# GpSimd's expert stage of a hybrid decoder layer written out for 64 experts, with index columns read in place

## The reference

```python
combine = jnp.einsum('tk,tke->te', gate, jax.nn.one_hot(expert_idx, N_EXPERTS, dtype=f32)).astype(x.dtype)
y = jnp.einsum('tf,fd->td', jax.nn.silu(xt @ ws_gate) * (xt @ ws_up), ws_down)
for c in range(N_EXPERTS // EXPERT_CHUNK):
    sl = slice(c * EXPERT_CHUNK, (c + 1) * EXPERT_CHUNK)
    g = jnp.einsum('td,edf->tef', xt, w_gate[sl])
    u = jnp.einsum('td,edf->tef', xt, w_up[sl])
    hdn = jax.nn.silu(g) * u * combine[:, sl, None]
    y = y + jnp.einsum('tef,efd->td', hdn, w_down[sl])
x = layer_norm(ALPHA * x + ffn + ple, ln2_g[i], ln2_b[i])
```

## Time and profile before

| | us |
|---|---|
| median of 3 runs | 1579.32 |
| lowest and highest run | 1578.99, 1583.84 |
| span of the profiled execution | 1578.7 |
| PE busy in it | 1434.9 |
| POOL busy in it | 463.6 |

### The profile page before, as it was taken

How to read it: one execution, slowest core, us unless ns; L and a number is a source line. 1 busy time by engine, 2 the same in 40 slices (tenths; PEclk the granted TensorE clock), 3 DMA queues, 4 the chain that set the end, 5 groups by cost and what they waited for, 6 DMA issues and landing times.

```text
span 1578.7 us, 18524 instructions
## 1 busy us (share of the span) xinstructions
PE 1434.9 (91%) x6293; PEld 938.1 (59%) x6293; DVE 858.9 (54%) x1240; ACT 600.2 (38%) x847; POOL 463.6 (29%) x414
## 2 busy tenths in 40 slices
PE   7979797988999999999975999999999999999990
PEld 4457676666788888554433666555555655556550
DVE  4597857674800100345614666656666566565654
ACT  3115454444622222010012554545545545455440
POOL 2012434343444444000351322223232222222322
PEclk8999898989899999999997999999999999999996
DMA  8034242425133335720156899999999999999953
GB/s 236 0 108 80 68 68 67 68 54 107 54 106 91 97 96 171 300 116 1 32 211 222 295 348 344 340 341 335 346 334 333 343 338 336 339 327 339 335 163 119
DMA packets 141491, 315.97 MB, mean 200 GB/s; under 512 B 18898, under 2 KB 100514, under 8 KB 116160
## 3 DMA queue, kind: packets, MB, share of 16 engines
q1 hardware_dynamic: 125984, 281.50, 51.8%
q0 software_dynamic: 15456, 33.79, 8.9%
HBM read 297.35 MB, written 34.65 MB: 210 GB/s over the span
## 4 chain that ended last, share of the span: by engine, by line
DMA 39%; PE 36%; issue 8%; DVE 5%; POOL 5%; ACT 2%; POOLq 2%; DVEq 1%; SPq 0%; ACTq 0%
DMA acc_dram<-arena 38%; PE bank L696 8%; PE bank L697 8%; PE bank L698 8%; PE bank L914 3%; PE bank L730 3%; POOL slot_dram L621 2%; DVE arena L1330 2%; PE bank L928 2%; PE bank L703 2%; POOL arena L643 2%; ACT arena L1111 1%; POOLq L587 1%; PE bank L829 1%; POOL arena L588 1%
## 5 line engine op out<-in xcount | busy, mean ns | idle before, releaser
L1330 DVE TENSOR_TENSOR gate_up_low<-gate_up,gate_up_high 128x1024 fp32r<-128x1024 f32 x256 | 296.4, 1221 | 228.6 <-ACT gate_up_high L1111 228.6
L1111 ACT ACTIVATE gate_up_high<-gate_up 128x1024 fp32r<-128x1024 f32 x256 | 249.5, 1047 | 215.5 <-DMA gate_up<-moe_w_up_in 198.8
L1111 ACT ACTIVATE arena<-bank 96x512 f32<-96x512 f32 (+5 forms) x248 | 130.7, 551 | 314.6 <-PE bank L1054 109.7
L696 PE MATMUL bank<-gate_up_high,rows_high 128*96 128x512 f32 x512 | 208.1, 406 | 26.5 <-DVE rows_low L1330 26.5
L1054 PE MATMUL bank<-down,arena 128*96 128x512 f32 x512 | 230.4, 592 | 1.0 <-DVE arena L1843 1.0
L1330 DVE TENSOR_TENSOR arena<-arena 128x512 f32<-128x512 f32 (+10 forms) x286 | 195.4, 715 | 46.5 <-POOLq L577 28.2
L698 PE MATMUL bank<-gate_up_high,rows_low 128*96 128x512 f32 x512 | 204.0, 398 | 0.0
L697 PE MATMUL bank<-gate_up_low,rows_high 128*96 128x512 f32 x512 | 202.7, 396 | 0.0
L703 PEld LDWEIGHTS bank<-arena 96*128 96x128 f32 (+4 forms) x1001 | 126.5, 192 | 115.9 <-DVE arena L1336 47.4
L703 PE MATMUL bank<-arena 96*128 96x96 f32 (+4 forms) x1001 | 134.8, 275 | 55.9 <-ACT arena L1111 29.4
L552 POOL TENSOR_TENSOR wb_low<-arena,wb_high 128x1024 fp32r<-128x1024 f32 (+1 forms) x40 | 105.9, 2647 | 150.9 <-ACT wb_high L1111 150.9
(11 more groups left out here) (149 smaller groups left out, 2132.0 us busy)
## 6 DMA issues: line engine op xcount, KB each, us to landing
gate_up<-moe_w_gate_in SPq DMA_DIRECT2D x64, 1024.0 KB, 14.2
gate_up<-moe_w_up_in SPq DMA_DIRECT2D x64, 1024.0 KB, 25.1
down<-moe_w_down_in SPq DMA_DIRECT2D x64, 1024.0 KB, 19.1
arena<-w_in_in SPq DMA_DIRECT2D x40, 512.0 KB, 4.2
arena<-w_glu_in SPq DMA_DIRECT2D x16, 512.0 KB, 4.0
arena<-w_lru_out_in SPq DMA_DIRECT2D x8, 768.0 KB, 5.0
arena<-x_in SPq DMA_DIRECT2D x8, 512.0 KB, 5.1
arena<-w_in_in SPq DMA_DIRECT2D x2, 2048.0 KB, 12.0
```

What stands on the lines that cost most here:

```text
L696: mm(dst, w_hi, v_hi, start=start, stop=False)
L1111: return nc.scalar.activation(out_, in_, func, **kw)
L1330: return V_.tensor_tensor(out_, a, b_, op)
```

## The change

POOL's instruction list for the 64 experts is written out, so e is a constant everywhere. Both indirect DMAs take their indices from `idxT[:, e:e + 1]`, and the 128 copies, the waits behind them and the counting of `col_seen` are gone. The waits for turned rows, for y and for the add before stay, as do the order of gathers and adds, the buffers, and all other engines' lists. The part for experts with more than 96 rows keeps a copied column.

```diff
-            def gather(e, u, n):
-
-                nc.gpsimd.tensor_copy(idxcol[:, u:u + 1].bitcast(i32), idxT[:, bass.ds(e, 1)].bitcast(i32)).then_inc(S["slot_col"], 1)
-                pool.wait_ge(S["slot_col"], n + 1)
-                pool.sem_inc(S["col_seen"], 1)
+            def gather(e):
                 nc.gpsimd.indirect_dma_start(
-                    out=xg[u], out_offset=None, in_=x1_dram,
-                    in_offset=bass.IndirectOffsetOnAxis(ap=idxcol[:, u:u + 1].bitcast(u32), axis=0),
-                    bounds_check=T - 1, oob_is_err=False).then_inc(s_gath[u], 16)
-
-            def add_rows(buf, e, n):
-
-                wait(pool, S["rows_added"], 16 * n)
-                pool.sem_inc(S["col_seen"], 1)
-                nc.gpsimd.tensor_copy(idxcol[:, 4:5].bitcast(i32), idxT[:, bass.ds(e, 1)].bitcast(i32)).then_inc(S["sc_col"], 1)
-                pool.wait_ge(S["sc_col"], n + 1)
-                pool.sem_inc(S["col_seen"], 1)
+                    out=xg[e % 4], out_offset=None, in_=x1_dram,
+                    in_offset=bass.IndirectOffsetOnAxis(ap=idxT[:, e:e + 1].bitcast(u32), axis=0),
+                    bounds_check=T - 1, oob_is_err=False).then_inc(s_gath[e % 4], 16)
+
+            def add_rows(e):
+                pool.wait_ge(S["y_e_act"], e + 1)
+                pool.wait_ge(S["y_e_dve"], e + 1)
+                if e:
+                    pool.wait_ge(S["rows_added"], 16 * e)
                 nc.gpsimd.indirect_dma_start(
-                    out=acc_dram, out_offset=bass.IndirectOffsetOnAxis(ap=idxcol[:, 4:5].bitcast(u32), axis=0),
-                    in_=yb[buf], in_offset=None, bounds_check=T - 1, oob_is_err=False,
+                    out=acc_dram, out_offset=bass.IndirectOffsetOnAxis(ap=idxT[:, e:e + 1].bitcast(u32), axis=0),
+                    in_=yb[e % 2], in_offset=None, bounds_check=T - 1, oob_is_err=False,
                     compute_op=ALU.add).then_inc(S["rows_added"], 16)
...
-            for u in range(4):
-                pool.wait_ge(S["xT_e_put"], u + 1)
-                gather(4 + u, u, 4 + u)
-                if u:
-                    add_expert(0, u - 1)
-            with pool.Fori(1, E // 4 - 1) as i:
-                for u in range(4):
-                    pool.wait_ge(S["xT_e_put"], 4 * i + (u + 1))
-                    gather(4 * i + (4 + u), u, 4 * i + (4 + u))
-                    add_expert(i, u - 1)
-            for u in range(E - 4, E):
-                add_expert(0, u - 1)
-            add_expert(0, E - 1)
+            for e in range(E):
+                if e + 4 < E:
+                    pool.wait_ge(S["xT_e_put"], e + 1)
+                    gather(e + 4)
+                if e:
+                    add_rows(e - 1)
+            add_rows(E - 1)
```

More of the change, by code:

```diff
@@ L653, in _, with over_gather, over_add @@
             pool.wait_ge(S["ple_done"], TT)
-            for u in range(4):
-                gather(u, u, u)
+            for e in range(4):
+                gather(e)
             pool.wait_ge(S["acc_stored"], 16)
[L658 to L661, removed]
-            for u in range(4):
-                pool.wait_ge(S["xT_e_put"], u + 1)
-                gather(4 + u, u, 4 + u)
-                if u:
-                    add_expert(0, u - 1)
-            with pool.Fori(1, E // 4 - 1) as i:
-                for u in range(4):
-                    pool.wait_ge(S["xT_e_put"], 4 * i + (u + 1))
-                    gather(4 * i + (4 + u), u, 4 * i + (4 + u))
-                    add_expert(i, u - 1)
-            for u in range(E - 4, E):
-                add_expert(0, u - 1)
-            add_expert(0, E - 1)
+            for e in range(E):
[5 more added lines that the diff above has]
+            add_rows(E - 1)
+            def over_gather(i):
+                nc.gpsimd.tensor_copy(idxcol[:, 0:1].bitcast(i32), idxT[:, bass.ds(i + E, 1)].bitcast(i32)).then_inc(S["slot_col"], 1)
+                pool.wait_ge(S["slot_col"], i + 1)
+                pool.sem_inc(S["col_seen"], 1)
+                nc.gpsimd.indirect_dma_start(
+                    out=xg[0], out_offset=None, in_=x1_dram,
+                    in_offset=bass.IndirectOffsetOnAxis(ap=idxcol[:, 0:1].bitcast(u32), axis=0),
+                    bounds_check=T - 1, oob_is_err=False).then_inc(s_gath[0], 16)
+            def over_add(i):
+                pool.wait_ge(S["rows_added"], 16 * i + 16 * E)
+                pool.sem_inc(S["col_seen"], 1)
+                nc.gpsimd.indirect_dma_start(
+                    out=acc_dram, out_offset=bass.IndirectOffsetOnAxis(ap=idxcol[:, 0:1].bitcast(u32), axis=0),
+                    in_=yb[0], in_offset=None, bounds_check=T - 1, oob_is_err=False,
+                    compute_op=ALU.add).then_inc(S["rows_added"], 16)
             n_over = pool.value_load(novi[0:1, 0:1].bitcast(i32), min_val=0, max_val=OV)
@@ L679, in _ @@
                     with pool.If(i < n_over):
-                        gather(i + E, 0, i + E)
+                        over_gather(i)
                         pool.wait_ge(S["o_y_kept"], 2 * i + 2)
-                        add_rows(0, i + E, i + E)
+                        over_add(i)
                         pool.wait_ge(S["rows_added"], 16 * i + 16 * (E + 1))
```

## The result

The changed kernel takes 1584.49 us (median of 17 runs) beside 1580.45 us for the kernel before (17 runs on the same chips): ratio 1.0024, 95% interval 1.0013 to 1.0036. It is slower by some 3.8 us (2.1 to 5.7), which is inside the 0.3% that were called "no change" and more than the 0.65 us that were forecast. The time of 1584.49 us lies half a microsecond above the forecast range. Part of that is the base: the forecast added its sum to 1579.32 us, the median of 3 runs, and the median of 17 is 1.1 us higher. But the 3.8 us, too, are more than the 2.5 us at which the forecast's sum ended. One of the 17 executions of the changed kernel took 5959.57 us; the median counts it and the ratio leaves it out. The profiled execution took 1583.0 us, its span is 1581.2 us.

What follows compares the result with a forecast made beforehand. The prediction took the weight loads on some 11 busy DMA engines as the bound. It added -1.35 us (end) and +2.0 us (one more add), +0.65 us, to the 1579.32 us median: 1579.9 us, range 1574.0 to 1584.0.

Steps and rivals of the forecast that it cites:

- What bounds the stage: Expert stage: weight loads on the slowest DMA engines set the 10.92 us interval; POOL's add, 39% of the chain, does not.
- 11 engines: DMA in the expert stage: some 11 of 16 engines carry all gather and add rows and are never idle.
- The reaction time of 0.9 us: POOL: time from a satisfied wait to the start of an indirect DMA; 0.9 us taken, between 0 and 1.80.
- The end: Last two adds, 62 and 63: with the lag gone, the last landing comes 1.35 us earlier.
- The price of catching up: Busy DMA engines carry one more add before the last weights land: 2.0 us taken, lower end 0.
- The interval stays 10.92 us, the gain here is 0: Mid-stage: earlier adds gain 0, since y and then the weights are late next.
- Gathers are worth 0, hidden behind the weights: Mid-stage: removing the gathers' 64 copies of 0.68 us gains 0, as PE needs a gather only several rounds later.
- The first: Rival: idle DMA slots come from the late add; an earlier add saves at most 0.76 us per expert, 1541 us; chance 0.13.
- The second: Rival: the lag stays, or goes without moving the weights; no price, end gains 1.35 us, 1578.0 us; chance 0.33.
- The third: Rival: an instruction fetch of POOL's straight-line list stalls the last two adds, 1585.2 to 1589.1 us; chance 0.09.
- The rule on who excludes whom: DVE instructions with two SBUF inputs and GpSimd SBUF reads exclude each other; if valid for indirect DMAs, adds stay locked behind DVE.
- The sum: Whole kernel: -1.35 us at the end plus 2.0 us for catching up, +0.65 us; ends -3.15 and +2.5.

Runs made afterwards that it cites:

- spread_before: Kernel before, with each expert's 96 slots reordered so that empty slots fall on all DMA engines alike; ratio to the kernel before 0.9722.
- the two groups above: Seven kernels with every transfer kept, by time from expert 9 to 15: kernel before and three others 63.9 to 64.6 us, changed kernel and two others 68.4 to 69.7.
- adds_on_old_beat2: Changed kernel, where each add (experts 1 to 57) also waits for DVE's low split of expert e + 3; ratio to the kernel before 1.0005.
- gathers_in_place: Changed kernel with the copied index column put back for the adds alone, gathers reading theirs in place; ratio to the kernel before 1.0003.
- unrolled_with_copies: Changed kernel, list still written out, but with both index copies and their waits put back; ratio to the kernel before 1.0013.
- the two held kernels: Changed kernel with adds also waiting for the next expert's y, for experts 1 to 57 or 13 to 57; ratios to the kernel before 1.0050 and 1.0030.
- adds_held_a_round: Changed kernel, where the adds of experts 1 to 57 also wait for y of the next expert; ratio to the kernel before 1.0050.
- gathers_mid_round: Changed kernel, with each gather held until the next expert's rows are turned, in the middle of the round; ratio to the kernel before 1.0123.

## Why the prediction was wrong

**What bounds the stage: right.** POOL's add, 39% of the chain, was worth nothing by itself. The weight loads set the pace, and with the empty slots spread the interval fell to 10.09 us (spread_before). That it is 11 engines fits the share of 0.71, but the price by omission (0.69 to 1.05 us, forecast 2.1) does not confirm the number.

**The reaction time of 0.9 us: right.** Row 1206.10 gives 0.85 us after y, and an indirect DMA behind another on POOL starts after 0.30 us.

**The end: right.** Chain of the kernel after:

```profile
1543.43 5.11 DMA acc_dram<-arena
...
1549.46 5.49 DMA acc_dram<-arena
1555.01 3.24 DMA arena<-acc_dram
```

Add 62 starts 0.82 us after its y (1541.92 + 0.69), add 63 starts 0.92 us after the landing. From the start of the last y copy to the last landing it is 8.2 us; it was 9.75. The gain is 1.5 us, where 1.35 were forecast, and 1.7 us to the end of the span. The last landing, 1554.95, lies within the 3 us allowed, but by luck: the stage began 4.1 us earlier in this execution, and counted from the first y copy the last add lands 6.8 us later than in the kernel before. The sign "last y copy up to 2 us later than 1542.48" failed: it starts at 1546.73.

**The price of catching up: the step that failed.** The forecast paid for it once, as one more add of 23.1 engine-us on 11 engines, 2.0 us. An add measured by omission costs 0.7 to 1.05, with the reservation made above. With that price the forecast's sum would have been -0.65 to -0.3 us, so this is not where the loss comes from. The 2.0 us were all that the forecast had for the stage, with 0 for its middle. What the stage really pays is 6.1 us on the mean of the two groups above: 68.80 - 64.23 = 4.6 at experts 9 to 15 and 44 x (10.993 - 10.937) = 2.5 after that, of which some 0.9 comes back in the last four.

It is not the number of transfers, since adds_on_old_beat2 has the same ones. The forecast let POOL catch up by 0.9 us an expert at no cost on the way. In the trace it catches up over experts 9 to 14, and the three kernels that do so lose 4.6 us there against the four that do not. How much of the 4.6 us is the one add and gather more, and how much their way through the middle of the round, is not shown.

**"The interval stays 10.92 us, the gain here is 0": wrong by its assumption.** A transfer's price was taken as fixed, so moving it could cost nothing as long as nobody waited for it. The interval became 11.00. In the stage's middle the same transfers run in every round of both kernels, and for the DMA engines only their time in the round differs. That such a shift has a price is shown for the gather by itself: with it in mid-round the interval is 11.394 us.

**"Gathers are worth 0, hidden behind the weights": wrong in the same way.** Their copies are worth 0 (gathers_in_place). But the gather stands behind the add on POOL, so moving the add moved it too, and by omission a gather costs no less than an add. The forecast named the gather as queued behind the waiting add and asked only who waits for it.

**The rivals.** The first, idle slots filled by an earlier add, is refuted: the interval rose. The second, lag gone without moving the weights, is refuted by the same number. The third, a fetch stall, is refuted: 33 fetch packets as before, and unrolled_with_copies keeps the old pace. None of them had a loss from the place in the round, which is why the range ended too low. The rule on who excludes whom (the Trainium skill, SBUF — State Buffer, Who interferes with whom) was weighed for the indirect DMA, which it does not hold here. For the copy the trace agrees with it (0.75 us up to the end of the split's last instruction, 0.18 outside), and that was the half which mattered: the held copy kept the adds on their beat. The forecast saw the hold and took its end for a saving.

**The sum.** Stage +6.1 (means of 0 to 63: 677.57 and 671.47), end -1.7: +4.4 us, where 0.0024 x 1580.45 = 3.8 us were timed, with an interval of 2.1 to 5.7. The first pair of profiles alone (8.35 - 1.7) would have said too much.

**What stays open.** The runs show that the loss comes when the adds and gathers leave their old beat and goes when they are put back on it. They do not show how an earlier add makes weight packets longer. The lag alone is not separated from the place in the round, since the two held kernels also made y wait. The mean over 16 engines is no full measure of it. The weights' queue of adds_held_a_round from 1050 to 1450 us:

```profile
q1 hardware_dynamic: 15910, 115.86, 76.8%
```

That is 0.309 us each, at an interval of 10.933 that its lead from the first rounds helps. Nor do the runs split the one loss at experts 9 to 13 between add and gather. A kernel with the add early and the gather at its old place was not run.

## What to carry to other kernels

Where a stage is bound by DMA engines, ask of every transfer not only who waits for it but when in the round it runs and what it runs beside; taking away a small instruction can move two large transfers. A wait that costs nothing can be worth keeping, because it holds a transfer at a cheap time. And when the mean DMA share stays below 1 in a stage that waits for its loads (0.93 here, and 0.71 in the dip of a round), look at how the bytes are spread over the engines first: here that gained 2.8%, and the change studied lost 0.24%.

## What the runs showed of the hardware that was not expected

- Moving a gather of 64 rows by 4.3 us within a round of 11 us, with nobody waiting for it, cost 0.4 us a round (gathers_mid_round).
- An add into memory takes 9.1 us to land, but leaving one out gained only 0.7 to 1.05 us, no more than leaving out a gather (1.25 us).
- A list of 128 indirect DMAs written out ran no differently from a loop: 33 fetch packets either way.
- A 96x1 copy on GpSimd took up to 0.95 us instead of 0.18 when it fell into the last instruction of VectorE's two-input split, and ended with it; such a hold fixed where in the round two large transfers ran.
